# Four-layer hybrid decoder on one NeuronCore: the stick-breaking layer in six panels, a weight split at another place in the norm updates, and no slope tables

## What is computed

```python
def reference(x, norm_g, ...):
    h = x
    for layer in range(DEPTH):
        kind, j = layer % N_MIXERS, layer // N_MIXERS
        u = rms_norm(h, norm_g[layer, 0])
        ...   # nsa_mixer, stick_breaking_mixer or swa_sink_mixer by kind
        h = h + rms_norm(u, norm_g[layer, 1])
        u = conv_ffn(rms_norm(h, norm_g[layer, 2]), ...)
        h = h + rms_norm(u, norm_g[layer, 3])
    return h
```

```python
s_w = jnp.einsum('btgrd,blgd->bgrtl', qb, kw).astype(f32) * scale - slopes[:, :, None, None] * dist_w
```

## Time and profile before

| | |
|---|---|
| median of 3 runs | 2695.88 us (2695.68 to 2696.88) |
| the profiled execution | 2692.94 us |
| its span, first to last instruction | 2691.2 us |
| TensorE busy | 2576.8 us (96%) |
| VectorE busy | 1652.7 us (61%) |
| ScalarE busy | 1178.2 us (44%) |
| GpSimd busy | 354.6 us (13%) |
| HBM read, written | 207.02 MB, 2.10 MB |

### The profile page before, as it was taken

How to read it: one execution, slowest core, us unless ns; L and a number is a source line. 1 busy time by engine, 2 the same in 40 slices (tenths; PEclk the granted TensorE clock), 3 DMA queues, 4 the chain that set the end, 5 groups by cost and what they waited for, 6 DMA issues and landing times.

```text
span 2691.2 us, 38440 instructions
## 1 busy us (share of the span) xinstructions
PE 2576.8 (96%) x13432; PEld 2176.4 (81%) x13432; DVE 1652.7 (61%) x2869; ACT 1178.2 (44%) x1827; POOL 354.6 (13%) x298
## 2 busy tenths in 40 slices
PE   8989999999999889999999999999999899999997
PEld 6879978888878567888878878888779898788886
DVE  7567667665363857777355767764376675676733
ACT  4356544443232745444234544442333664444431
POOL 1012221110010002111010021110010121211100
PEclk9999999999999999999999999999999999999999
DMA  4400023322233012332322023323333000233321
GB/s 156 135 30 2 1 85 104 101 94 95 79 106 94 16 49 86 94 98 81 111 75 71 21 84 101 100 94 97 96 103 101 17 2 32 86 95 96 99 94 55
DMA packets 62054, 210.93 MB, mean 78 GB/s; under 512 B 8673, under 2 KB 10465, under 8 KB 61921
## 3 DMA queue, kind: packets, MB, share of 16 engines
q1 hardware_dynamic: 61920, 209.14, 24.6%
HBM read 207.02 MB, written 2.10 MB: 78 GB/s over the span
## 4 chain that ended last, share of the span: by engine, by line
PE 84%; DVE 12%; ACT 2%; issue 1%; DMA 0%; DVEq 0%; POOL 0%; SPq 0%; ACTq 0%; POOLq 0%
PE psum L304 20%; PE psum L305 20%; PE psum L306 20%; PE psum L1073 6%; PE psum L1063 3%; PE psum L917 2%; PE psum L918 2%; PE psum L919 2%; DVE left L1910 2%; PE psum L1053 2%; PE psum L1052 2%; PE psum L338 1%; DVE h L516 1%; DVE w_lo L266 1%; DVE xl L497 1%
## 5 line engine op out<-in xcount | busy, mean ns | idle before, releaser
L304 PE MATMUL psum<-xh,w_hi 128*128 128x512 f32 x1736 | 678.6, 391 | 4.6 <-DVEq L979 3.7
L305 PE MATMUL psum<-xh,w_lo 128*128 128x512 f32 x1736 | 677.3, 390 | 0.0
L306 PE MATMUL psum<-xl,w_hi 128*128 128x512 f32 x1736 | 676.9, 390 | 0.0
L266 DVE TENSOR_TENSOR w_lo<-w_raw,w_hi 128x1024 fp32r<-128x1024 f32 x226 | 288.7, 1291 | 520.5 <-ACT w_hi L260 518.8
L260 ACT ACTIVATE w_hi<-w_raw 128x1024 fp32r<-128x1024 f32 x226 | 235.5, 1057 | 572.9 <-PE psum L306 450.6
L304 PEld LDWEIGHTS psum<-xh,w_hi 128*128 128x128 f32 x1736 | 326.7, 188 | 73.5 <-DVEq L979 4.1
L306 PEld LDWEIGHTS psum<-xl,w_hi 128*128 128x128 f32 x1736 | 326.7, 188 | 67.6
L305 PEld LDWEIGHTS psum<-xh,w_lo 128*128 128x128 f32 x1736 | 326.7, 188 | 66.9
L720 DVE TENSOR_TENSOR w_lo<-w_raw,w_hi 128x1024 fp32r<-128x1024 f32 x160 | 209.2, 1308 | 253.6 <-ACT w_hi L716 253.6
L305 PE MATMUL psum<-ah,w_lo 128*128 (+1 forms) x704 | 274.2, 389 | 0.0
L304 PE MATMUL psum<-ah,w_hi 128*128 (+1 forms) x704 | 274.2, 389 | 0.0
(11 more groups left out here) (193 smaller groups left out, 3870.9 us busy)
## 6 DMA issues: line engine op xcount, KB each, us to landing
w_raw<-w_up SPq DMA_DIRECT2D x176, 512.0 KB, 3.6
w_raw<-w_down SPq DMA_DIRECT2D x88, 512.0 KB, 3.6
w_raw<-nsa_in SPq DMA_DIRECT2D x56, 512.0 KB, 3.9
w_raw<-sb_in SPq DMA_DIRECT2D x24, 512.0 KB, 3.7
w_raw<-nsa_out SPq DMA_DIRECT2D x16, 512.0 KB, 3.6
w_raw<-swa_in SPq DMA_DIRECT2D x10, 512.0 KB, 3.7
w_raw<-sb_out SPq DMA_DIRECT2D x8, 512.0 KB, 3.6
w_raw<-swa_out SPq DMA_DIRECT2D x8, 512.0 KB, 3.7
```

Of the source, the lines that this page charges most:

```text
L266: nc.vector.tensor_tensor(w_lo[:, u % RING, :], w_raw[:, u % RING, :], w_hi[:, u % RING, :].bitcast(F32), ALU.subtract).then_inc(split_don ...
L304: nc.tensor.matmul(bank(p, o), wh[:, k, o, :], xhi(k), start=(first and k == 0), stop=False)
L305: nc.tensor.matmul(bank(p, o), wl[:, k, o, :], xhi(k), start=False, stop=False)
L306: mm = nc.tensor.matmul(bank(p, o), wh[:, k, o, :], xlo(k), start=False, stop=(last and k == 1))
```

## The change

1. SB gets six panels: the unused one, `stays`, `late_u` and its copies go, and every update now reads the last four chunks from PSUM. All panels behind it change their half. A function `half_of` puts the scores, transposes and outputs of the SB and SWA layers on the other half (`k ^ 4`), and leaves the NSA layers as they are.
2. In the update, ScalarE's split of the fourth unit moves from ahead of `xh` of chunk 0 to behind the square of chunk 1; VectorE's from behind `low(3)` to behind `low(2)`, ahead of `update(0)`.
3. The tables `tb` go. The query is divided by the head's slope when it is split, L1121 adds the plain distance and multiplies the sum by the slope (its `scale`, a constant, 1.0 before). GpSimd keeps only `add`. The loads of `slopes` for the SWA layer and two bookkeeping semaphores go.

The core of the diff:

```diff
-MIX_PANELS = {"nsa": 8, "sb": 7, "swa": 3}
+MIX_PANELS = {"nsa": 8, "sb": 6, "swa": 3}
...
         def dve_sum_squares(dve, s):
-            def take(o):
-                if not stays(s):
-                    dve.wait_ge(sq_done, 8 * s + 5 + o)
-                    nc.vector.tensor_copy(late_u[:, o, :], bank(p, o)).then_inc(u_done, 1)
...
@@ dve_update
             def update(c):
                 if c < 4:
                     src, d = u[:, c, :], dh[:, c % 2, :]
-                elif stays(s):
+                else:
                     src = d = bank(p, c - 4)
-                else:
-                    src, d = late_u[:, c - 4, :], dh[:, c % 2, :]
...
             update(3)
             low(2)
+            split_lo(dve, u_split)
             update(0)
             for c in range(4, DC):
                 dve.wait_ge(h_done, 8 * s + c)
                 update(c)
                 low(c - 1)
-                if c == 4:
-                    split_lo(dve, u_split)
             low(DC - 1)
...
@@ act_update
             for k, c in enumerate((1, 2, 3, 0, 4, 5, 6, 7)):
                 act.wait_ge(h_done, 8 * s + k + 1)
                 if c:
                     high(c)
                 square(k, c)
+                if k == 0:
+                    split_hi(act, u_split)
...
+        def half_of(l, k):
+            return k if kinds[l] == "nsa" else k ^ 4
...
@@ the query's split, VectorE (its ScalarE half gets scale=1.0 / slope(R * it + r))
-                nc.vector.tensor_tensor(qs[d_, r % 2, :], qt[s_, bass.ds(it * 2 + r // 2, 1), :],
-                                        qs[s_, r % 2, :].bitcast(F32), ALU.subtract).then_inc(qs_ready, 1)
+                nc.vector.scalar_tensor_tensor(qs[d_, r % 2, :], qt[s_, 2 * it + r // 2, :], 1.0 / slope(R * it + r),
+                                               qs[s_, r % 2, :].bitcast(F32), ALU.mult, ALU.subtract).then_inc(qs_ready, 1)
@@ biased
-                if i == TC - 1 and b == 0:
-                    dve.wait_ge(tb_done, it * R + (h0 + R * w + r + 1))
-                x = nc.vector.tensor_tensor_reduce(out=sp_[:, s % 4, 0:nk * P], in0=psum[:, s % 4, 0:nk * P], in1=bias,
-                                                   scale=1.0, ...
+                x = nc.vector.tensor_tensor_reduce(out=sp_[:, s % 4, 0:nk * P], in0=psum[:, half_of(l, s % 4), 0:nk * P], in1=away,
+                                                   scale=slope(R * (it + w) + r), ...
...
@@ main program, ScalarE
                     act_rn(act, ch, 2 * l, plan.out_p[l] + 1)
-                    split_hi(act, plan.up_u[l] + AHEAD)
-                    act_update(act, 2 * l, 4 * l + 2)
+                    act_update(act, 2 * l, 4 * l + 2, plan.up_u[l] + AHEAD)
```

More of the change, by code:

```diff
@@ L447, in dve_take_u, with dve_sum_squares @@
                 nc.vector.tensor_copy(u[:, o, :], bank(p, o)).then_inc(u_done, 1)
-            dve.wait_ge(u_done, 4 * (s + 1) + 4 * sum(not stays(x) for x in range(s)))
+            dve.wait_ge(u_done, 4 * (s + 1))
             dve.sem_inc(evac_v, 1)
-        def dve_sum_squares(dve, s, p):
-            def take(o):
-                if not stays(s):
-                    dve.wait_ge(sq_done, 8 * s + 5 + o)
-                    nc.vector.tensor_copy(late_u[:, o, :], bank(p, o)).then_inc(u_done, 1)
+        def dve_sum_squares(dve, s):
             dve.wait_ge(ss_done, s + 1)
@@ L862, in hybrid_layers @@
         qs_ready = sem("qs_ready")
-        tb_done = sem("tb_done")
         s_done = sem("s_done")
@@ L906, in sp_mixer @@
             elif kind == "swa":
-                for dst, src in ((dist, "dist_w"), (slopes, "slopes"), (sinks, "sinks")):
+                for dst, src in ((dist, "dist_w"), (sinks, "sinks")):
                     sp.dma_start(dst[:], ins[src]).then_inc(mix_landed, 16)
@@ L1049, in scores @@
                 cols = slice(k0 * P, (k0 + nk) * P)
-                out_ = psum[:, s % 4, 0:nk * P]
+                out_ = psum[:, half_of(l, s % 4), 0:nk * P]
                 kg = bass.ds(it + w, 1) if w or not isinstance(it, int) else slice(it, it + 1)
@@ L1072, in values @@
                     for j in range(nk):
-                        mm = nc.tensor.matmul(psum[:, 6 + job % 2, i * (DH + 1):(i + 1) * (DH + 1)], pt[:, s % 2, j * P:(j + 1) * P],
+                        mm = nc.tensor.matmul(psum[:, half_of(l, 6 + job % 2), i * (DH + 1):(i + 1) * (DH + 1)], pt[:, s % 2, j * P:(j + 1) * P],
                                               vt[b][:, k0 + j, it, :], start=(j == 0), stop=(j == nk - 1),
@@ L1240, in act_attention, with slope @@
             act.wait_ge(om_done, OM_FREE + jobs_before[l + 1])
+        def slope(head):
+            return float(np.float32(2.0 ** (-8.0 * (head + 1) / H)))
         def esink_bias(it, r):
@@ L1777, in scores @@
                         s_ = slice(64 * a, 64 * a + 64)
-                        mm = nc.tensor.matmul(psum[:, (s + a) % 4, at_:at_ + (i + 1) * P], sq_t[s_, e // 2, i * P:(i + 1) * P],
+                        mm = nc.tensor.matmul(psum[:, half_of(l, (s + a) % 4), at_:at_ + (i + 1) * P], sq_t[s_, e // 2, i * P:(i + 1) * P],
                                               sk_t[s_, e // 2, 0:(i + 1) * P], start=True, stop=True, skip_group_check=True)
```

99 lines of the change are left out of this document (32 added, 67 removed).

## The result

The changed kernel takes 2680.14 us (median of five runs, 2679.54 to 2686.28), the kernel before 2695.88 (2695.33 to 2696.88). The ratio is 0.9948, 95% interval 0.9933 to 0.9962: faster, by 0.5%. The profiled run of the changed kernel is its slowest, 2686.28 us with a span of 2684.5. Run once more beside the experiments it took 2678.42 (2675.31 to 2680.49) against 2695.93 (2691.12 to 2699.74 in 17 runs), ratio 0.9934 (0.9921 to 0.9947), and I use that second profile (span 2678.0) too.

The account below looks back on a forecast made before the run. VectorE was taken to bound the norm updates up to chunk 4, TensorE behind it. Gains 6.0 + 3.5 + 2.0 less 0.8 make 10.7 us off the median 2695.88: 2685.2 us, range 2680.5 to 2691.5.

Parts of the forecast that it names:

- The bound and the mechanism: Norm updates between sublayers: VectorE bounds them up to chunk 4, TensorE behind it; the split takes 2.31 us against a median 1.226.
- The split on VectorE: Norm updates: moving the split ahead of chunk 0's update gains 1.2 us in five updates, 6.0 us (2.5 to 7.8).
- what is late next: Norm updates: chunk 3's `xl` comes 1.2 us later, so TensorE waits there and a little at chunk 4.
- The clock at c4: Third update: the clock fell at chunk 4, costing 1.56 us more than its like; half of that counted as gain.
- rival 1: Norm updates: up to five clock drops come onto the path at up to 1.56 us each, 2690 to 2693; chance 0.12.
- The split on ScalarE: Start of each norm update: TensorE can start 0.55 us sooner, but the move is costed at nothing.
- The second update: Update before the stick-breaking layer: six panels give 2.3 us and the moved split 1.2, together 3.5 (2.8 to 4.2).
- The copies: Four copies to `late_u`, forced by the skipped panel: they mostly lay beside TensorE work.
- The third: Third norm update: 1.2 us plus half of 1.56 from the clock drop, 2.0 us gained (0.5 to 3.1).
- The other PSUM half: Everything behind the dropped panel: flipped parity keeps order and waits; cost nothing, bounds 0.2 us either way.
- No slope tables: Sliding-window loop: `qs` with a factor takes 0.065 us more, 13 times, 0.8 us slower (0 to 1.1); NSA loops hide it.
- L332 to L386 takes some 23.5 us: Sign of being right: the window from first `xh` matmul to sum of squares takes this in every update.

## Why the prediction was right or wrong

- **The bound and the mechanism** (VectorE sets c4, the split is stretched by GpSimd): right. Undoing that one move costs 12.5 us, most of the gain.
- **The split on VectorE, 1.2 per update, 6.0 in all**: too large. Measured 0.63 to 0.70 in each of the five ordinary updates, 3.4 in all. Up to c4 the step came out: `w_lo` 1.22, c3's `xl` 1.21, c4's `xl` products 16.65 us behind the first `dh` for a forecast of 16.5 and 17.76 before. What failed is the answer to "what is late next": it names c3 and "again a little at c4" and stops there. GpSimd, which starts 1.14 us later, also ends later, and c5's `xl` goes from 0.74 to 1.83. So c5's products come 3.14 us behind c4's and not near 2.72, and of the 1.11 us gained at c4 some 0.4 are given back behind it.
- **The clock at c4**: rival 1 expected that drops would come onto the path. They left it: 11 of 26 updates with the old place, none of 41 with the new. The sum prices this at half of 1.56 for the third update alone, where it was a chance of some 0.4 in each of six (an estimate: six times 0.4 times 1.56 is 3.7 for a priced 0.8). This miss is as large as the one on the split, and it went the other way.
- **The split on ScalarE, nothing**: right by its own run (2680.00 for 2678.42, updates equal), with the start 0.62 sooner for a forecast of 0.55.
- **The second update, 3.5**: 3.03, within its bounds. **The copies, hidden**: right by the run without the counter, where the FFN with them takes 338.50; the 0.38 us in the kernel before need the idle time ahead of them too. **The third, 2.0**: 2.25.
- **The other PSUM half, nothing**: nothing seen. The runs hold it against seven panels only together with the rest; it was not changed alone, so this stays argued.
- **No slope tables, 0.8 slower**: wrong in sign, some 3.7 us faster, 2 of them in the sliding-window layer. This was the largest miss of a single term. Two steps failed. `qs` with a factor takes 0.686, as without; I had taken it to be like the 128x512 instructions with a pointer for a factor:

```profile
L1084 DVE SCALAR_TENSOR_TENSOR qs<-qt,qs x48: 684/686/690, 169.2 to 2230.5; 64x512 fp32r<-64x512 f32 x48
```

  And I listed the table, its product and its wait, but not the `sem_inc` that the diff removes in front of every score instruction. It has no row in any busy-time view, and it was the only part of the loop that mattered. In the NSA loops, which the prediction held safe because VectorE waits for TensorE there, it cost 0.84 us each.
- **"L332 to L386 takes some 23.5 us"**: wrong even for a gain of 1.2, because the same text lets the window start 0.55 sooner.
- **The sum, 10.7**: the accounted parts come to 8.7 (updates), 3.7 (counter) and 0.4 (that FFN), 12.8. The medians differ by 15.7 and, in the second comparison, 17.5. The rest fits the clock drops that the one profile of before happened to have few of: it has one at c4, where 11 of 26 make two or three, and the kernel without the counter has three and a drop in the second update, and sums to 211.36 for its updates instead of 207.30. That fits and is not shown. A sum made against one profile misses what varies from run to run.
- **The range**: that it nearly holds the result is partly luck. The split was forecast 2.6 us too high, the clock drops and the counter 3 and 4.5 too low, and a range of 11 us took in the balance. (Its bounds also count the 0.2 of the other half upward only: the low gain is 4.5 and not 4.7.)

## What to carry to other kernels

When an instruction is moved out of the way of another engine, follow that other engine to its end too: here GpSimd's later start met another of VectorE's instructions and took back 0.4 of 1.1 us, and starting it later still, by one wait, gave 1.1 us per update. That version, 2675.24 us, ratio 0.9910, is the fastest measured here, though the one with c3 first as well (0.9928) lies within the noise of it. Count what a diff removes that has no busy time (semaphore increments, waits) wherever an engine's queue is the bound. And measure with a mark that neither version moves.

## What was not expected of the hardware

- With an increment of a semaphore by itself in front of it on VectorE's queue, a score instruction started 0.22 us behind the read ahead of it, and 0.04 without. It cost 0.13 us per head in the sliding-window loop and 0.84 us per NSA layer in 24 reciprocals' time.
- The same line, gone from the attention loops, took with it 0.31 us of idle time ahead of a sum in a feed-forward layer. Its cause is open.
- With the split in its old place the clock fell in 25 of 26 updates, either at c0 or at c4 and never at both; only at c4 did it cost time (1.5 us).
- The same program had its clock low for 10 or for 17 us at the start of the same loop, and an NSA layer's time followed the low time from 335 to 341 us.
- In one order of the update the clock stayed low for 34 us while TensorE was busy without a pause. Its cause is open.
